# A two-layer transformer block: where the first two weight tiles stand in the load order, and two positions per compression matmul

## The reference

```python
mod = c @ w_ada[l] + b_ada[l]
sh1, sc1, gt1, sh2, sc2, gt2 = jnp.split(mod, 6, axis=-1)
h = rms_norm(x, g_pre_mix[l]) * (1.0 + sc1[:, None]) + sh1[:, None]
proj = h @ w_in[l]
...
def compress(kv, pe, w1, w2):
    B, T, G, dh = kv.shape
    n_cmp = (T - CMP_LEN) // CMP_STRIDE + 1
    blk = np.arange(n_cmp)[:, None] * CMP_STRIDE + np.arange(CMP_LEN)[None, :]
    blocks = kv[:, blk] + pe[None, None, :, None, :]
    flat = blocks.transpose(0, 1, 3, 2, 4).reshape(B, n_cmp, G, CMP_LEN * dh)
    return jax.nn.gelu(flat @ w1) @ w2
```

## Time and profile before

| | |
|---|---|
| median of three runs | 1918.88 us (1916.68 to 1921.71) |
| the profiled execution | 1921.35 us |
| its span in the trace | 1919.5 us |
| mean granted TensorE clock, share of full | 0.978 |
| TensorE busy | 1828.1 us (95%) |
| VectorE, ScalarE, GpSimd busy | 935.1, 697.7, 134.1 us |
| transfers | 176.15 MB, mean 92 GB/s |

### The profile page before, as it was taken

One profiled execution on the slowest core, in us unless ns is written; L12 is line 12 of the kernel. 1 busy time (PEld: TensorE's weight loads), 2 busy tenths in 40 slices (PEclk: granted clock), 3 DMA queues, 4 the chain that ended last, 5 costly groups with the idle time before them and its releaser, 6 DMA issues.

```text
span 1919.5 us, 27690 instructions
## 1 busy us (share of the span) xinstructions
PE 1828.1 (95%) x11652; PEld 1423.4 (74%) x11652; DVE 935.1 (49%) x1482; ACT 697.7 (36%) x1055; POOL 134.1 (7%) x109
## 2 busy tenths in 40 slices
PE   5998989989999998999999999899888899999999
PEld 2666655758888887788888887666688688888887
DVE  4276877364344343544344544545755544433442
ACT  4224557343223233432133334577311433312321
POOL 0013435200000002000000010000000010000000
PEclk8998998989999999999999999999999999999999
DMA  9662101113222223223223322111000122322241
GB/s 380 241 237 105 47 28 34 66 44 99 99 99 96 92 98 99 66 92 129 66 99 107 102 77 77 57 43 44 23 4 4 67 94 93 123 85 88 98 126 40
DMA packets 44475, 176.15 MB, mean 92 GB/s; under 512 B 5568, under 2 KB 5824, under 8 KB 41024
## 3 DMA queue, kind: packets, MB, share of 16 engines
q1 hardware_dynamic: 44352, 174.38, 26.8%
HBM read 168.33 MB, written 2.10 MB: 89 GB/s over the span
## 4 chain that ended last, share of the span: by engine, by line
PE 86%; DVE 7%; ACT 3%; DMA 3%; issue 2%; SPq 0%; DVEq 0%; ACTq 0%
PE bank L365 24%; PE bank L366 23%; PE bank L367 23%; PE bank L509 2%; PE bank L525 1%; PE bank L541 1%; PE bank L716 1%; DMA arena<-ada 1%; PE bank L857 1%; PE bank L874 1%; PE bank L865 1%; DMA arena<-ada_late 1%; PE bank L435 1%; DMA ring<-m_w_v 1%; ACT wsp L1088 1%
## 5 line engine op out<-in xcount | busy, mean ns | idle before, releaser
L1563 DVE TENSOR_TENSOR wsp<-ring,wsp 128x1024 fp32r<-128x1024 f32 (+2 forms) x244 | 313.7, 1287 | 442.6 <-ACT wsp L1088 442.5
L365 PE MATMUL bank<-hs,wsp 128*128 128x512 f32 x1160 | 473.1, 408 | 16.1 <-DVE hs L1830 5.3
L1088 ACT ACTIVATE wsp<-ring 128x1024 fp32r<-128x1024 f32 (+2 forms) x244 | 268.7, 1103 | 579.4 <-PE bank L367 573.7
L367 PE MATMUL bank<-hs,wsp 128*128 128x512 f32 x1160 | 455.5, 393 | 0.0
L366 PE MATMUL bank<-hs,wsp 128*128 128x512 f32 x1160 | 455.3, 393 | 0.0
L365 PEld LDWEIGHTS bank<-hs,wsp 128*128 128x128 f32 x1160 | 220.2, 190 | 87.4 <-issue 31.5
L366 PEld LDWEIGHTS bank<-hs,wsp 128*128 128x128 f32 x1160 | 220.3, 190 | 48.9 <-issue 5.9
L367 PEld LDWEIGHTS bank<-hs,wsp 128*128 128x128 f32 x1160 | 219.7, 189 | 47.2
L365 PE MATMUL bank<-hids,wsp 128*128 128x512 f32 x608 | 236.5, 389 | 0.0
L366 PE MATMUL bank<-hids,wsp 128*128 128x512 f32 x608 | 236.5, 389 | 0.0
L367 PE MATMUL bank<-hids,wsp 128*128 128x512 f32 x608 | 236.5, 389 | 0.0
(11 more groups left out here) (340 smaller groups left out, 2116.0 us busy)
## 6 DMA issues: line engine op xcount, KB each, us to landing
ring<-m_gate SPq DMA_DIRECT2D x44, 512.0 KB, 3.4
ring<-m_up SPq DMA_DIRECT2D x44, 512.0 KB, 3.4
ring<-m_down SPq DMA_DIRECT2D x32, 704.0 KB, 4.1
ring<-m_w_in SPq DMA_DIRECT2D x38, 512.0 KB, 3.5
arena<-ada_late SPq DMA_DIRECT2D x16, 1024.0 KB, 5.8
ring<-m_w_up SPq DMA_DIRECT2D x32, 512.0 KB, 3.4
ring<-m_w_down SPq DMA_DIRECT2D x32, 512.0 KB, 3.4
ring<-m_w_out SPq DMA_DIRECT2D x16, 512.0 KB, 3.6
```

The lines of the kernel that those rows point to most:

```text
L365: pe.matmul(out, lhs[0], rhs[0], start=start, stop=False)
L367: return pe.matmul(out, lhs[1], rhs[0], start=False, stop=stop)
L1088: act.activation(wsp[:, s % SPLIT, 0, 0:size], ring[:, i % RING, 0:size], ACT.Copy)\
L1563: dve.tensor_tensor(wsp[:, s % SPLIT, 1, 0:size], ring[:, i % RING, 0:size], wsp[:, s % SPLIT, 0, 0:size].bitcast(F32), ALU.subtract).then ...
```

## The change

There are two edits.

First, `w_v` tile 0 was issued behind piece k = 5 of `ada` and tile 1 behind piece k = 7; now both are issued behind k = 7.

Second, a compression matmul takes two positions. `w1` is laid out with positions 2l and 2l + 1 in the two halves of the partitions, so that there are 16 matmuls in place of 32 and two tiles of 512 KB in place of three of 704 KB. A position of each parity has to be in its half of the partitions for both groups; the half that lies on the wrong side is brought over by `swap_halves`, two transfers of 64 rows for keys and two for values, counted by a new semaphore `moved` (which also counts the stores of the output at the end). GpSimd waits for them, and makes eight operations of 64 x 8 x 31 in place of four of 64 x 16 x 31. SP's second swap also waits for GpSimd's key blocks. The buffer of the moved halves, `other_half`, lies in the half of the old `blk` that the new one leaves free. The tile table `after` is shifted to fit the shorter stream: `w_in` 10 now stands where the third key tile stood, and `w_in` 11 is no longer behind the wait for `compress(0)`.

```diff
--- before.py
+++ after.py
@@ -89,7 +89,7 @@
                   ("g_post_ffn", 8), ("norm_ffn1_2", 8), ("norm_mix_2", 8), ("norm_ffn2_2", 8),
                   ("sb_q", 1), ("sb_k", 1), ("sb_out", 4), ("rw_mu", 14), ("rw_w0", 4), ("rw_a0", 4),
                   ("rw_k_k", 4), ("rw_k_a", 4), ("rw_r_k", 4), ("rw_ln_w", 4), ("rw_ln_b", 4),
-                  ("pe_k", 32), ("pe_v", 32)]:
+                  ("pe_k", 16), ("pe_v", 16)]:
     COLS[_name] = (_at, _at + _n)
     _at += _n
 NCOLS = _at
@@ -110,8 +110,8 @@
 def weight_stream():
 
     out = [("w_v", n, 4 * VCOLS) for n in range(2)]
-    out += [("w_in", n, 8 * P) for n in range(10)] + [("cmp1k", n, SLOT) for n in range(3)]
-    out += [("w_in", n, 8 * P) for n in range(10, 12)] + [("cmp1v", n, SLOT) for n in range(3)]
+    out += [("w_in", n, 8 * P) for n in range(10)] + [("cmp1k", n, 8 * P) for n in range(2)]
+    out += [("w_in", n, 8 * P) for n in range(10, 12)] + [("cmp1v", n, 8 * P) for n in range(2)]
     out += [("w_in", n, 8 * P) for n in range(12, 16)]
     out += [("w_out", n, 8 * P) for n in range(8)]
     for q in range(FF1_PARTS):
@@ -230,7 +230,8 @@
         QI, KI, KC, VC, KSL, KW, QN, QD, KDD = 0, 2, 3, 4, 5, 6, 7, 11, 15
 
         oalt, _ = at("oalt", [P, 16, T], F32R, arena_at + 4 * 18 * K)
-        blk = area(66 * K, (CMP_L, 2, CMP_N))
+        blk = area(66 * K, (CMP_L // 2, 2, CMP_N))
+        other_half = area(70 * K, (2, T))
         kcmp = area(4 * K + 128, (CMP_N,))
         vcmp = area(5 * K, (2, 4 * DH))
         cs = area(7 * K, (2, HEADS, CMP_N))
@@ -476,13 +477,13 @@
 
             def compress(m):
 
-                ws = [take_whole("cmp1" + "kv"[m], "cmp_hid", m + 1).rearrange("p (l m) -> p l m", m=P) for _ in range(3)]
+                ws = [take_whole("cmp1" + "kv"[m], "cmp_hid", m + 1).rearrange("p (l m) -> p l m", m=P) for _ in range(2)]
                 pe.wait_ge(S("cmp_blocks"), m + 1)
                 if m == 0:
                     claim(6, "cmp_gelu", 1)
-                for l in range(CMP_L):
-                    mm = pe.matmul(bank[:, 6, 2 * CMP_N * m:2 * CMP_N * (m + 1)], ws[l // 11][:, l % 11, :],
-                                   blk[:, l, :, :].rearrange("p g n -> p (g n)"), start=(l == 0), stop=(l == CMP_L - 1))
+                for l in range(CMP_L // 2):
+                    mm = pe.matmul(bank[:, 6, 2 * CMP_N * m:2 * CMP_N * (m + 1)], ws[l // 8][:, l % 8, :],
+                                   blk[:, l, :, :].rearrange("p g n -> p (g n)"), start=(l == 0), stop=(l == CMP_L // 2 - 1))
                 mm.then_inc(S("cmp_hid"), 1)
 
             def cmp_keys():
@@ -2199,17 +2200,20 @@
             for m in range(2):
                 src, pe_name = ((KC, "pe_k"), (VC, "pe_v"))[m]
                 pool.wait_ge(S("roped"), src + 1)
+                pool.wait_ge(S("moved"), 32 * (m + 1))
                 if m:
                     pool.wait_ge(S("cmp_hid"), 1)
                 for half in range(2):
                     for g in range(2):
-
-                        rows = slice(DH * g, DH * g + DH)
-                        v = proj[rows, src, 16 * half:16 * half + 16 * 31].rearrange("p (n l) -> p l n", l=16)
-                        pe_b = vec(pe_name, 16 * half, 16)[rows, :, None].to_broadcast([DH, 16, 31])
-                        ins = pool.tensor_tensor(blk[rows, 16 * half:16 * half + 16, g, 0:31], v, pe_b, ALU.add)
-                        if half + g < 2:
-                            do(ins)
+                        for s in range(2):
+
+                            rows = slice(DH * s, DH * s + DH)
+                            v = proj[rows, src, :] if s == g else other_half[rows, m, :]
+                            v = v[:, 16 * half:16 * half + 16 * 31].rearrange("p (n l s) -> p l s n", l=8, s=2)[:, :, s, :]
+                            pe_b = vec(pe_name, 8 * half, 8)[rows, :, None].to_broadcast([DH, 8, 31])
+                            ins = pool.tensor_tensor(blk[rows, 8 * half:8 * half + 8, g, 0:31], v, pe_b, ALU.add)
+                            if half + g + s < 3:
+                                do(ins)
                 ins.then_inc(S("cmp_blocks"), 1)
                 own("cmp_blocks")
 
@@ -2264,8 +2268,8 @@
                 if k >= 4:
                     sy.wait_ge(S(f"ada_in{k % 4}"), 16)
                 sy.dma_start(ada_in[k], ada[k]).then_inc(S(f"ada_in{k % 4}"), 16)
-                if k in (5, 7):
-                    tile_load(k // 2 - 2)
+            tile_load(0)
+            tile_load(1)
             sy.wait_ge(S("ada_in1"), 32)
             tile_load(2)
             sy.dma_start(cst[:, NFIRST:], consts[:, NFIRST:]).then_inc(S("consts"), 16)
@@ -2278,9 +2282,18 @@
                     sy.dma_start(ropet[32 * b:32 * b + 32, n % 2, :], ropein[32 * (b ^ 1):32 * (b ^ 1) + 32, n % 2, :])\
                       .then_inc(S(f"turned{n % 2}"), 16)
 
+            def swap_halves(m):
+                src = (KC, VC)[m]
+                sy.wait_ge(S("roped"), src + 1)
+                if m:
+                    sy.wait_ge(S("cmp_blocks"), 1)
+                for s in range(2):
+                    sy.dma_start(other_half[DH * s:DH * s + DH, m, :], proj[DH * (1 - s):DH * (1 - s) + DH, src, :])\
+                      .then_inc(S("moved"), 16)
+
             place = {tile[:2]: i for i, tile in enumerate(STREAM)}
             after = {n: ("w_in", n + 7) for n in range(3)}
-            after.update({3: ("cmp1k", 0), 4: ("cmp1k", 1), 5: ("cmp1k", 2), 6: ("w_in", 10), 7: ("cmp1v", 2),
+            after.update({3: ("cmp1k", 0), 4: ("cmp1k", 1), 5: ("w_in", 10), 6: ("w_in", 11), 7: ("cmp1v", 1),
                           8: ("w_in", 15), 10: ("w_out", 0), 11: ("w_out", 1), 12: ("w_out", 2), 13: ("w_out", 3)})
             pieces = {0: 4, 1: 6, 2: 8, 4: 10, 5: 12, 6: 14}
             for i in range(3, 7):
@@ -2295,6 +2308,8 @@
                     late_load(pieces[n])
                 if n != VC:
                     turn_halves(n)
+                if n - 1 in (KC, VC):
+                    swap_halves((KC, VC).index(n - 1))
                 if n in pieces:
                     late_load(pieces[n] + 1)
                 while n in after and i <= place[after[n]]:
@@ -2305,8 +2320,8 @@
                 i += 1
             for n in range(KD):
                 sy.wait_ge(S("x_added"), 4 * KD + n + 1)
-                sy.dma_start(out[:, n * T:(n + 1) * T], x[:, n, :]).then_inc(S("stored"), 16)
-            sy.wait_ge(S("stored"), 16 * KD)
+                sy.dma_start(out[:, n * T:(n + 1) * T], x[:, n, :]).then_inc(S("moved"), 16)
+            sy.wait_ge(S("moved"), 64 + 16 * KD)
 
 
 
@@ -2335,10 +2350,8 @@
     mats = {"w_in": tiles(feat),
             "w_v": np.ascontiguousarray(tok.reshape(2, 4, P, VCOLS).transpose(0, 2, 1, 3).reshape(2, P, 4 * VCOLS))}
     for name in ("k", "v"):
-        w1 = f["cmp_w1_" + name][0].reshape(CMP_L, DH, P).transpose(1, 0, 2)
-        w1 = np.concatenate([w1, w1], 0)
-        w1 = np.concatenate([w1, np.zeros((P, 1, P), np.float32)], 1)
-        mats["cmp1" + name] = np.ascontiguousarray(w1.reshape(P, 3, SLOT).transpose(1, 0, 2))
+        w1 = f["cmp_w1_" + name][0].reshape(CMP_L // 2, 2 * DH, P).transpose(1, 0, 2)
+        mats["cmp1" + name] = np.ascontiguousarray(w1.reshape(P, 2, 8 * P).transpose(1, 0, 2))
     w_out = f["w_out"][0]
     paired = w_out[0:512].reshape(2, 4, DH, D).transpose(1, 0, 2, 3).reshape(512, D)
     mats["w_out"] = tiles(np.concatenate([paired, w_out[512:]], 0))
@@ -2363,7 +2376,7 @@
     cols += [columns(pair(f["sb_q_norm_2"][0])), columns(pair(f["sb_k_norm_2"][0])), columns(f["sb_out_norm_2"][0])]
     cols += [columns(f[n][0]) for n in ("rw_mu_2", "rw_w0_2", "rw_a0_2", "rw_k_k_2", "rw_k_a_2", "rw_r_k_2",
                                         "rw_ln_w_2", "rw_ln_b_2")]
-    cols += [np.concatenate([f["cmp_pe_" + n][0].T] * 2, 0) for n in ("k", "v")]
+    cols += [f["cmp_pe_" + n][0].reshape(CMP_L // 2, 2 * DH).T for n in ("k", "v")]
     cols = np.ascontiguousarray(np.concatenate(cols, 1))
     lora = np.concatenate([f["rw_w2_2"][0], f["rw_a2_2"][0]], 0)
     extra = np.ascontiguousarray(np.concatenate([lora, f["rw_g2_2"][0], f["cmp_w2_k"][0], f["cmp_w2_v"][0]], 1))
```

## The result

The change makes the kernel slower, by a little under 1%. The median went from 1917.78 us (1913.96 to 1921.71, 4 runs in alternation with the changed kernel) to **1936.14 us** (1932.68 to 1937.48, 4 runs): a ratio of 1.0092, 95% interval 1.007 to 1.0114, or +17.6 us (13.4 to 21.9). The forecast was 1916.1 with a range up to 1921.5, so the result lies well outside it, on the side to which I had given 0.02. The profiled execution after took 1937.27 us beside a span of 1935.5 (1919.5).

What follows compares the result with a forecast made beforehand. TensorE, holding 86% of the chain, was taken as the bound; -3.6 + 0.6 + 0.2 = -2.8 from the median 1918.88 gave 1916.1 us, counted as no change, range 1912.0 to 1921.5.

Steps and rivals of the forecast that it cites:

- two of them: Both compression products pay: -6.4, 1912.5 us, chance 0.10; the first tiles move the modulation-row copy: 1915.0 to 1917.5, chance 0.07.
- a wait of VectorE's: Rotation beside GpSimd's value blocks: at 1.34 us a piece VectorE's chain is late, 2.7 us of gain gone, 1918.8; chance 0.08.
- a stop of SP's queue: Second swap waits for key blocks, delaying late piece 13 and lowering TensorE's clock: +3.2, 1922.1 us; chance 0.10.
- the chance of "slower": Whole kernel: slower by over 0.3%, above 1924.7 us, was given 0.02.
- Order of the first tiles: Start: ScalarE's copy of the modulation rows stays at 36.2 us, cost 0; bounds -1.1 and +1.4.
- First compression: First compression product, on the chain from 133.97 us: 32 of 64 TensorE records go, all of it counting, -3.6 us.
- Second compression: Second compression product, from 151.33 us: TensorE's 3.6 us gain is waited off because VectorE sets the time, 0.
- Swap ahead of late piece 13: SP's queue: the second pair of swap transfers delays late piece 13's issue to 117.8, TensorE waits +0.6 us.
- the cover of 1.4 us: Key blocks: swap lands after 4.3 us, blocks ready at 115.1, SP looks at 116.5, so 1.4 us to spare.
- the second rival: The stop of SP's queue: GpSimd's small pieces no cheaper, blocks ending at 121.2; +3.2, 1922.1 us, chance 0.10.
- GpSimd's blocks: Key and value blocks: eight pieces at 0.89 us, 7.1 against 5.4 us, ready before they are wanted, cost 0.
- VectorE's lock: VectorE's rotation beside GpSimd's value blocks: its three operations each wait for GpSimd's SBUF reads, taken as +0.2 us.

Runs made afterwards that it cites:

- the kernel before with the 128 bytes alone: The kernel before with 128 unused bytes ahead of `ext`, so that `ext`, `tmp` and `arena` move: 1938.13 us, ratio 1.0085.
- old addresses: The changed kernel with `ext` aligned to 512 bytes, so `ext`, `tmp` and `arena` stand where they did in the kernel before: 1915.63 us, ratio 0.9973.
- the compression alone: The changed kernel with `ext` aligned to 512 bytes and the first two weight tiles where they were before: 1915.28 us, ratio 0.9987.
- the order alone: The kernel before with only the first edit, both `w_v` tiles issued behind the eighth piece: 1920.65 us, ratio 0.9996.
- the four kernels of the table: The changed kernel, the one with old addresses, the late swap and the compression alone; from ScalarE's copy 8 to 9: 22.24, 22.21, 22.24 and 22.08 us.
- the three with the old one: The kernel before, the same with 128 bytes ahead of `ext`, and the order alone; from ScalarE's copy 8 to 9: 21.10, 21.10 and 21.11 us.
- the late swap: The changed kernel with `ext` aligned to 512 bytes and the second swap moved from ahead of late piece 13 to behind late piece 15: 1913.88 us, ratio 0.9962.

## Why the prediction was wrong

**The step that failed** is the first paragraph's: "the Tensor work after the first 300 us is not touched". The instructions are not touched; their operands' addresses are. The hunk on the column table was read as bookkeeping and costed at nothing, without a bound. It costs 15.7 us by the work on the three tiles, 0.85% (0.55 to 1.16) or 16 us by the kernel before with the 128 bytes alone. None of the rivals had it: two of them moved the sum within the gain, one was a wait of VectorE's, and the one that came out slower was a stop of SP's queue. So the chance of "slower" was 0.02 where one unpriced hunk stood open. Without the 128 bytes the time is 1915.63, which the forecast of 1916.1 would have met, though in part by luck: VectorE's lock cost 1.0 us where it had 0.2, and the gain against the kernel before is uncertain by 4 us either way.

The steps on which the sum rested, one by one:

- **Order of the first tiles, 0: right.** The copy came at 35.89 and 36.12, and TensorE waited 4.25 us for it in place of 1.7. Ratio 0.9996 alone. (The rate of 425 KB a us in its working is some 415 by its own figures, 2,744 KB in 6.6 us, which changes no term.)
- **First compression, -3.6: right**, 3.79 us for 32 records, 3.5 less.
- **Second compression, 0: right.** It ran 151.07 to 154.8, and a TensorE wait of 1.70 us for VectorE's `smin` (L1733) followed at 158.40.
- **Swap ahead of late piece 13, +0.6: right in one execution, too low in two.** With old addresses TensorE waited 0.45, 0.27 and 0.84 us where it had waited 0.91: +0.65. In the profile of the compression alone the waits were 0.55, 0.59 and 1.00: +1.2. With the order alone, which has no swap, they came to 1.63 (0.73 at an earlier piece, and 0.90), so 0.7 us is within what one profile differs from another. In the changed kernel's profile the swap landed after 6.7 us in place of the 4.3 that I took, and the cover of 1.4 us was gone: a wait of 2.33 us and 1.3 us (0.58 and 0.73) for the slow piece and scores behind it, less the old 0.91: +2.7. This is the second rival's mechanism with a dear landing instead of dear pieces, and one of the prediction's own signs of being wrong: a wait above 2 us at late piece 13 with the lower clock behind it. The addresses don't enter here.
- **GpSimd's blocks, 0.89 us a piece: right** (0.91 and 0.94), but not for nothing. The prediction asked when SP and TensorE want the blocks, not what stands behind them on GpSimd; that is the next point.
- **VectorE's lock, +0.2: right mechanism, wrong place.** The rotation of group 7 lost 0.84 us and had cover for it. The index scores lost 1.02 us (2.64 against 1.62) and had none: 8 to 9 grew from 21.10 to between 22.08 and 22.24 in the four kernels of the table that have the new compression with its product behind group 7, while the three with the old one kept 21.1. The index scores begin 3.2 us behind ScalarE's copy of group 8, as they did (3.0). It is GpSimd's rotation of group 8 that comes later, 2.2 us behind that copy in place of 0.7, since eight small value blocks take 7.55 us where four large ones took 5.77, and it runs into them.

By the terms as measured the edits are worth -3.5 + 0.65 + 1.0 = -1.9 us, in place of -2.8. The aligned kernel shows -0.27% or -5.2 us (-9.0 to -1.3), the compression alone -2.5 (-4.8 to 0), the late swap -7.3 (-10.2 to -4.6). The signs agree with the terms; the late swap's interval lies beyond them, and where its last microseconds come from is open: its profile has them ahead of group 1 and behind group 9, where the same instructions varied by 3 and by 6.6 us from one profile to the next.

The sum of it all, -1.9, +2 from the slow landing where it happens, and 15.7 to 16.3 from the addresses, is some +16, beside a measured +17.6 (13.4 to 21.9).

Open are the mechanism behind the distance (the runs tell which addresses, not what inside the memory or TensorE collides), whether it holds for other shapes than 128x512 and for types other than fp32r (the float32 groups above showed none), and whether a loss of this kind has other periods than 256 bytes.

## What to carry to other kernels

A hunk that changes the size of any tile moves everything allocated behind it: before costing it at nothing, compare the addresses of the tiles that TensorE streams and loads, not only the lists of instructions. In this kernel it pays to fix streamed tiles and weights at the same address modulo 256 (one alignment: 1936 to 1916 us). And when an engine's work gets longer, ask what stands behind it in that engine's own list, not only who waits for its result: GpSimd's longer blocks delayed its next operation by 1.5 us, into VectorE's index scores, where the lock had no cover.

## What the runs showed of the hardware

A 128x512 fp32r matmul whose streamed and loaded tiles stand 128 bytes apart modulo 256 takes longer than one whose tiles don't: 395 against 389 ns with `hids` streamed, 394 to 397 against 389 to 392 with `h2a`, 397 against 393 or 394 with `hs` (second and third pass of a product). For `hids` the spacing goes from 0.227 to 0.234 us (414.74 and 426.84 us for 1824). It follows the distance, from either side (`arena` + 128, `arena` - 128, `hs` + 128, `wsp` + 128 are all dear; `arena` + 256 and all + 128 are not), and some half of it is there at 64 bytes. It holds with the roles turned round (`wsp` streamed, `hs` loaded: 395 against 389), and the float32 matmuls of this kernel (`arena` streamed, `cst` loaded) show none of it. The load of the weights shows no difference (188 to 190 ns). Over this kernel it is 0.85% for the tiles in `arena`, 1.2% for `hs`, 1.5% for both.
